# Strassen's scheme for w_up in groups 2 to 7 of both MLPs, with its sums of h kept in DRAM and streamed back

## What is computed

```python
h = _rmsnorm(x, g_mlp[i]) * (1.0 + sc2[:, None, :]) + sh2[:, None, :]
u = jnp.square(jax.nn.relu(jnp.einsum('bsd,df->bsf', h, w_up[i])))
x = x + gt2[:, None, :] * jnp.einsum('bsf,fd->bsd', u, w_down[i])
...
u = rms_norm(h, norm_mlp[l])
h = h + jnp.square(jax.nn.relu(u @ w_up[l])) @ w_down[l]
```

## Time and profile before

| | us |
|---|---|
| median of 3 runs | 2766.41 (2764.86 to 2769.73) |
| the profiled execution | 2768.58 |
| its span, first to last instruction | 2766.8 |
| PE busy | 2582.5 (93%) |
| DVE busy | 1701.5 (61%) |
| POOL busy | 1247.7 (45%) |
| ACT busy | 972.8 (35%) |
| mean granted clock of TensorE | 0.967 |

### The profile page before, as it was taken

How to read it: one execution, slowest core, us unless ns; L and a number is a source line. 1 busy time by engine, 2 the same in 40 slices (tenths; PEclk the granted TensorE clock), 3 DMA queues, 4 the chain that set the end, 5 groups by cost and what they waited for, 6 DMA issues and landing times.

```text
span 2766.8 us, 36836 instructions
## 1 busy us (share of the span) xinstructions
PE 2582.5 (93%) x14368; PEld 2106.0 (76%) x14368; DVE 1701.5 (61%) x2304; ACT 972.8 (35%) x1566; POOL 1247.7 (45%) x784
## 2 busy tenths in 40 slices
PE   4988988899999999999999999789699999999998
PEld 4866866677778888888887768667588888888887
DVE  6268988864766655556635684477425556655554
ACT  4235366644243322222333442243305223322222
POOL 2432365444647566556632323323264456554441
PEclk8999999999999999999999999899699999999999
DMA  6201032001311110112213110000230211111111
GB/s 227 69 8 31 24 100 84 16 24 65 127 54 61 54 40 28 61 61 61 65 31 107 39 38 31 1 2 2 94 97 31 61 61 61 45 31 45 61 61 61
DMA packets 142500, 153.50 MB, mean 55 GB/s; under 512 B 7183, under 2 KB 105252, under 8 KB 142374
## 3 DMA queue, kind: packets, MB, share of 16 engines
q1 hardware_dynamic: 137088, 143.97, 16.3%
q10 hardware_dynamic: 5286, 7.79, 0.8%
HBM read 143.35 MB, written 8.39 MB: 55 GB/s over the span
## 4 chain that ended last, share of the span: by engine, by line
PE 78%; DVE 12%; ACT 5%; issue 4%; DMA 1%; POOL 0%; ACTq 0%; SPq 0%; DVEq 0%; POOLq 0%
PE ps L2389 19%; PE ps L2115 11%; PE ps L2117 11%; PE ps L2116 11%; PE ps L2130 4%; PE ps L2131 4%; PE ps L2132 4%; ACT sel_out L1048 2%; PE ps L2547 2%; PE ps L2206 2%; DVE yt L1941 2%; DVE yt L1930 1%; PE ps L2284 1%; PE ps L2098 1%; PE ps L2273 1%
## 5 line engine op out<-in xcount | busy, mean ns | idle before, releaser
L757 POOL TENSOR_TENSOR w_lo<-raw,w_hi 128x1024 fp32r<-128x1024 f32 x170 | 447.9, 2641 | 560.1 <-ACT w_hi L1181 559.5
L2115 PE MATMUL ps<-h_hi,w_hi 128*128 128x512 f32 x1472 | 585.6, 398 | 8.8 <-issue 4.3
L2116 PE MATMUL ps<-h_lo,w_hi 128*128 128x512 f32 x1472 | 575.3, 391 | 0.0
L2117 PE MATMUL ps<-h_hi,w_lo 128*128 128x512 f32 x1472 | 575.0, 391 | 0.0
L2115 PEld LDWEIGHTS ps<-h_hi,w_hi 128*128 128x128 f32 x1472 | 278.1, 189 | 76.3 <-issue 16.4
L1181 ACT ACTIVATE w_hi<-raw 128x1024 fp32r<-128x1024 f32 x162 | 171.7, 1060 | 435.0 <-PE ps L2389 363.9
L2116 PEld LDWEIGHTS ps<-h_lo,w_hi 128*128 128x128 f32 x1472 | 278.2, 189 | 59.9 <-issue 3.6
L2117 PEld LDWEIGHTS ps<-h_hi,w_lo 128*128 128x128 f32 x1472 | 277.9, 189 | 58.7
L1793 DVE SCALAR_TENSOR_TENSOR u_f<-ps,u_f 128x512 f32<-128x512 f32 x128 | 88.1, 688 | 371.6 <-ACT u_f L1178 371.6
L2389 PE MATMUL ps<-w_lo,us_hi 128*128 128x512 f32 x784 | 306.9, 391 | 0.0
L2389 PE MATMUL ps<-w_hi,us_hi 128*128 128x512 f32 x784 | 306.8, 391 | 0.0
(11 more groups left out here) (448 smaller groups left out, 4550.1 us busy)
## 6 DMA issues: line engine op xcount, KB each, us to landing
raw<-in_w_up_dram SPq DMA_DIRECT2D x64, 512.0 KB, 4.4
raw<-in_w_down_dram SPq DMA_DIRECT2D x64, 512.0 KB, 3.5
raw<-in_w_ada_dram SPq DMA_DIRECT2D x48, 512.0 KB, 3.8
raw<-in_w_in_dram SPq DMA_DIRECT2D x32, 512.0 KB, 3.8
raw<-in_w_out_dram SPq DMA_DIRECT2D x32, 512.0 KB, 3.5
...
```

Source lines behind the costliest of these rows:

```text
L757: g_.tensor_tensor(w_lo[:, slot, :], raw[:, r, :], w_hi[:, slot, :].bitcast(F32), ALU.subtract).then_inc(sem("split_done"), 1)
L2115: mm(ps[:, bank, :], wh, h_hi[:, k, cols], start=(k == 0), stop=False)
L2116: mm(ps[:, bank, :], wh, h_lo[:, k, cols], start=False, stop=False)
L2117: last = mm(ps[:, bank, :], wl, h_hi[:, k, cols], start=False, stop=(k == NK - 1))
```

## The change

In groups 2 to 7 of both MLPs the up phase is Strassen's scheme as well: w_up (two halves of channels by two halves of the group's hidden units) times h (two halves of channels by two halves of tokens), seven products of 24 matmuls, 168 instead of 192. Groups 0 and 1 (PLAIN = 2) keep the plain up phase.

- The sums of h are four *pieces* T1 to T4, each 512 channels by 512 tokens, in a high and a low part. They are made once for each MLP, during groups 0 and 1: POOL makes them (`whole`, `less`) in 32 instructions of 128x512, ACT copies the high parts (16), DVE subtracts the low parts (16), and ACT issues 32 DMAs that write them to h_t in DRAM.
- In each of groups 2 to 7 SP loads all four pieces again, 16 DMAs of 512 KB: T1 and T3 into the second half of h_hi and h_lo for four of the eight channel tiles, T2 and T4 into four extra buffers.
- The sums of w_up (S1 to S4) are four more `mix` of POOL for each group, and there are seven up items instead of four, so seven copies by ACT and seven subtractions by POOL. Two of the extra buffers take the fourth slot of w_hi and w_lo: from group 2 on weights have three slots.
- The results of the seven products are summed partly in PSUM and partly on DVE: ACT copies three pairs of banks to u_f (`copy_out`), DVE adds a later pair (`add_to`), ACT then does Relu and Square in place (`square`); the last quarter is Relu by ACT and a multiplication by DVE as before. All of it is 128x1024. Which quarter of u plays which part in the down phase changes with it (QUARTER).
- The loop over groups is written out on every engine, and group 7 keeps its plain down phase.

```diff
@@ tables @@
+        LAST, PLAIN = GROUPS - 1, 2
+        UP_ROLE = ("A11", "S1", "S2", "A12", "S3", "S4", "A22")
+        DOWN_ROLE = ("N11", "T1", "T2", "N22", "T3", "N21", "T4")
+        T_EVENTS = [("up", 0, b) for b in range(3, 8)] + [("down", 0, p) for p in range(7)]
+        T_EVENTS += [("up", 1, b) for b in range(8)] + [("down", 1, p) for p in range(4)]
@@ SP @@
+                for g in range(PLAIN, GROUPS):
+                    for c in range(4):
+                        load_piece(g, "T3", c, (g, 1))
...
+                    for c in range(4):
+                        load_piece(g, "T4", c, (g, 2))
...
+                            load_piece(g + 1, "T1", c, (g, 4))
...
+                            load_piece(g + 1, "T2", c, (g, 6))
@@ POOL @@
+                def pieces(c):
...
+                    for p in range(2):
+                        pool.wait_ge(sem(f"t_out{p}"), 256 * k + 64 * c)
+                    whole(ht[0], c, 1)
+                    whole(ht[1], c, 0)
+                    whole(ht[2], 4 + c, 1)
+                    summed(c, "b22")
+                    less(ht[1], ht[0], ht[1])
+                    less(ht[0], ht[2], ht[0])
+                    summed(c, "T1")
+                    less(ht[2], ht[2], ht[1])
...
+                    if g >= PLAIN:
+                        low(g, ("u", 0))
...
+                        mix(g, "S3", "A11", "A21")
...
+                        mix(g, "S1", "A21", "A22", ALU.add)
+                        low(g, ("u", 1))
+                        split_there(g, ("u", 1))
+                        mix(g, "S2", "A22", "S3")
+                        low(g, ("u", 2))
...
+                        mix(g, "S4", "A12", "S2")
+                        for i in range(3, 7):
+                            low(g, ("u", i))
@@ ACT @@
+                def square(g, name, quarter):
+                    squared_there(g, "a" + name)
+                    u = u_f[:, quarter, :]
+                    s.activation(u, u, ACT.Relu).then_inc(sem("u_act"), 1)
+                    acted(g, "r" + name)
+                    s.activation(u, u, ACT.Square).then_inc(sem("u_act"), 1)
...
+                def pieces(*event):
...
+                    for j in {1: (0,), 2: (1,), 4: (2, 3)}.get(step, ()):
+                        n = 4 * c + j
+                        act.wait_ge(sem("t_hi"), 16 * k + n + 1)
+                        act.dma_start(h_t[k, j, c, :, 0, :], ht_hi[j % 2].bitcast(F32)).then_inc(sem(f"t_out{j % 2}"), 16)
+                        act.wait_ge(sem("t_lo"), 16 * k + n + 1)
+                        act.dma_start(h_t[k, j, c, :, 1, :], ht_lo[PIECE_BUF[j]].bitcast(F32)).then_inc(sem(f"t_out{j % 2}"), 16)
+                    if step < 4:
...
+                        act.wait_ge(sem("t_sum"), n_sum(k, c, PIECES[step]))
+                        s.activation(ht_hi[step % 2], ht[PIECE_BUF[step]], ACT.Copy).then_inc(sem("t_hi"), 1)
@@ DVE @@
+                def add_to(g, p, need, quarter, bank):
+                    dve.wait_ge(sem("up_full"), n_up(k, g, p))
+                    acted(g, need)
+                    v.tensor_tensor(u_f[:, quarter, :], u_f[:, quarter, :], ps[:, bank:bank + 2, :],
+                                    ALU.add).then_inc(sem("u_sq"), 1)
@@ PE @@
+                def seven_up(g):
+                    A, B = (4, 0) if g == LAST else (0, 4)
+                    for p, (bank, where) in enumerate(((A, 0), (A + 2, "T1"), (A, "T2"), (B, 4), (A, "T3"), (A + 2, 4), (A, "T4"))):
+                        pe.wait_ge(sem("split_done"), m0 + ITEM[g, ("u", p)])
...
                 def product(g, p):
+                    pe.wait_ge(sem("split_done"), m0 + ITEM[g, ("d", p)])
+                    pe.wait_ge(sem("u_lo"), n_u(k, g, ("M11", "S1", "S2", "S4", "S3", "M12", "M22")[p]))
...
+                        elif p == 1:
+                            pe.wait_ge(sem("u_sq"), n_sq(k, g, "c21" if i < 2 else "a12"))
```

More of the change, by code:

```diff
@@ new lines, in build @@
+        UHI, UHI_N = tally(per_group(["S1", "M11", "S2", "S4", "S3", "M12", "M22"],
+                                     ["M11", "S1", "S2", "S4", "S3", "M12", "M22"],
+                                     ["c11", "c22", "c12", "c21"]))
+        ITEM, ITEM_N = tally([([("e", i) for i in range(4)] if g < PLAIN else [("u", i) for i in range(7)])
+                              + [("d", i) for i in range(4 if g == LAST else 7)] for g in range(GROUPS)])
+        LAST_ROLE = ("N11", "N21", "N12", "N22")
@@ new lines, in summed, with whole, less @@
+                def summed(c, name):
+                    pool.wait_ge(sem("t_sum"), n_sum(k, c, name))
+                def whole(dst, c, half):
+                    cols = slice(half * HALF, (half + 1) * HALF)
+                    g_.tensor_tensor(dst, h_hi[:, c, cols].bitcast(F32), h_lo[:, c, cols].bitcast(F32),
+                                     ALU.add).then_inc(sem("t_sum"), 1)
+                def less(dst, one, other):
+                    g_.tensor_tensor(dst, one, other, ALU.subtract).then_inc(sem("t_sum"), 1)
@@ L1835, in group @@
+                    pieces("down", g, 2)
                     out(g, 3)
-                    low(us_lo[0], u_f[:, A22, :], us_hi[0], n + 7)
-                    for p in range(4, PRODUCTS):
+                    low(g, "M22", us_lo[0], q["M22"], us_hi[0])
+                    pieces("down", g, 3)
+                    for p in range(4, 7):
                         out(g, p)
+                        pieces("down", g, p)
                 def down(n):
@@ L2425, in mlp @@
                 pe.wait_ge(sem("norm_hi"), base + NK)
[L2426 to L2428 removed]
+                up(0, 0, 0, nk)
+                up(0, 0, 1)
                 for u in range(NK, NK + 4):
```

781 lines of the change are left out of this document (535 added, 246 removed).

## The result

The changed kernel takes 2851.5 us (median of 4 runs, 2846.4 to 2858.2), the kernel before 2766.4 on the same chip: ratio 1.031, 95% interval 1.028 to 1.033. It is slower; 2856 was forecast. The profiled execution has a span of 2850.5 us, 83.7 more than the 2766.8 of before.

What follows compares the result with a forecast made beforehand. PE bounds the kernel, busy 82.0 of 82.0 us in a group. Group terms of 84.1, clock 14 and a correction of -8 give +90 on 2768.6, so 2859, or 2856 as median; 8-in-10 range 2785 to 2895 us.

Steps and rivals of the forecast that it cites:

- The removed product: One product of 24 matmuls gone from each of groups 2 to 7, both MLPs: 65.3 us, the whole possible gain.
- First MLP, groups 2 to 6: POOL's unbroken queue from u6 delays d2 to 60.4; group 87.9 us against 82.0, five groups +29.5 us.
- Second MLP: Groups 2 to 6: DVE is last, d1 starts at 47.1; group 81.3 us, five groups -3.5 us.
- The turns: POOL and DVE instructions on SBUF lock each other out: 2.38 and 1.1 us each; seven DVE turns add 7.7 us before d2.
- turns miss each other: Rival: POOL and DVE seldom meet in the new order, groups of 79.9 and 76.4 us, total 2736; chance 0.09.
- Groups 0 and 1: Making the pieces of h stands ahead of what PE needs: +36.2 us in the first MLP, +22.3 in the second.
- pieces hidden: Rival: work on the pieces fits POOL's idle time, groups 2 to 6 as forecast; 2794 us, chance 0.13.
- Group 7: 24 fewer matmuls, but the last quarter's low part comes late; stalls 4.5 and 6.5 us: -1.2 and +0.8 us.
- DMA: Loads of the pieces in each group arrive in time, DMA engines about half busy: 0 us.
- Clock: PE runs at half clock after new stalls: 1.0 us for each of 14 groups, 14 us; bounds nothing to 54.
- timetable correction: The timetable puts today's T4 and S4 low part 0.7 and 0.9 us late; 0.5 off for 16 groups, -8 us.
- The sum: Group terms 84.1 us, clock 14, correction -8: +90 us in all.

Runs made afterwards that it cites:

- keep_busy: Changed kernel plus throwaway matmuls of h (22 in the first MLP, 12 in the second) in TensorE's pause ahead of d1, groups 2 to 6: 2846.9 us.
- small_sums: Changed kernel with GpSimd's eight sums of w_up and w_down cut to 8 of 1024 columns, groups 2 to 6 and group 7's up half: 2798.1 us.
- next_orders: Changed kernel with GpSimd's and VectorE's orders changed in groups 2 to 6, plus three moves putting T3, N22's gate multiplication and S3 later: 2862.7 us.
- no_pieces: Changed kernel without the arithmetic of the pieces of h; the same bytes still written and loaded: 2797.3 us.
- last_only: Against the changed kernel: seven plain groups, only the last in seven products; pieces spread over four groups; plain groups' gates at group start: 2761.9 us.

## Why the prediction was right

- **The removed product** is removed (288 matmuls), and the groups' waits eat it, as forecast.
- **First MLP, groups 2 to 6.** Forecast: d1 at 50, d2 at 60.4, released by POOL, a group of 87.9, +29.5 in all. Measured: 49.4, 59.4, released by POOL, 88.1 in the mean, +30.4. That POOL's queue is the cause of d2's wait is shown by leaving out the gates (-6.3 us a group) and by changing POOL's order (-2.7).
- **Second MLP.** Forecast: d1 at 47.1, released by DVE's multiplication, 81.3 us, -3.5. Measured: 2473.70 - 2426.57 = 47.1, and 82.1 us, +0.4. The chain up to d1 is right. Behind d1 the forecast had 1.2 us for DVE's additions and the clock in its own term; measured is the half clock, 1.7 us, and the additions' share comes to light only when the clock is kept up (keep_busy: 81.4). They overlap, and do not add.
- **The turns.** The step that made the forecast go slower. small_sums shows it: with POOL's sums made small, DVE's unchanged sums go back to 1.22 us, and d1's wait nearly goes. In the first MLP POOL needs 32.8 us from the low part of u6 to that of d2, where eleven times 2.38 are 26.2: its turns cost 6.6 us, and 7.7 were put down. The rival "turns miss each other" is out.
- **Groups 0 and 1.** Forecast +36.2 and +22.3, without the clock; measured +36.1 and +22.0, with it. An agreement to 0.3 us is luck: the first MLP's two were put at 20.9 and 15.3 and are 19.0 and 17.1, and the same two groups take 3.5 us more in small_sums and next_orders, which do not touch them. One step is misread: the forecast lets the square of bank 7 release d1, at 57.2 in group 1 of the second MLP. It comes at 57.0, but bank 7 is the last quarter of d0, and d1 starts at 59.7. The rival "pieces hidden" (2794) is the time of no_pieces (2797), where their arithmetic is left out, and last_only shows that hiding them was open to the design, not to this order.
- **Group 7.** Forecast +0.8 and -1.2, with waits of 6.5 and 4.5 us. Measured +0.8 and +0.2, with waits of 4.2 and 3.7: the first is ended by POOL's low part for d0, the second by DVE's low part of the last quarter. Both waits were put too long; the half clock behind them makes up for it.
- **DMA.** 0 forecast; few_loads shows 0.9 us in the total and 0.1 in the ten groups.
- **Clock, the term that was mis-sized.** 1.0 us a group was put down. In the first MLP, 88.1 less 76.6 of matmuls and 7.4 of waits leaves 4.1 us; in the second 82.1 - 76.6 - 3.2 = 2.3, of which keep_busy gives 0.7 back in the mean and the products behind d1 take the rest. The waits themselves were shorter than forecast (7.4, not 11.3, in the first MLP) because d1, at half clock, takes 2 to 3 us of the time until d2 is released. The two errors cancel, and nothing in the forecast says that they should: with its share of the clock term and of the timetable correction the forecast for these ten groups is 26 + 10 - 5 = +31 us, the measurement +30.9.
- **The sum.** +90 forecast, +83.7 measured. The sixteen groups together give +90.0, which by the terms above is in part luck. The 6.3 between are the stretches that the change does not touch: +2.0 before the first MLP and -8.3 in the mixer behind it, at a higher clock. No term held them. In the traces of the other experiments that leave group 7 as it is, the stretch from the first MLP's last down half to the second MLP, 666.3 us here, took 666 to 675 us; what sets its clock stays open.
